# A two-layer audio trunk on one core: gates, norms and decays between the K, V and Q products, the output gate's products inside the chunk scan

## The reference

```
h = rms_norm(x, mix_norm_pre) @ mix_w_in          # Q,K,V,Z: 4 heads x 128 each; a,b: 4 each; conv part: 2 x 512
o_gdn = gated_deltanet_group(h, ...)
o_cm  = conformer_conv_group(h, ...)
x = x + rms_norm(concat([o_gdn, o_cm]) @ mix_w_out, mix_norm_post)

def gated_deltanet_group(h, conv_w, a_log, dt_bias, out_g):
    qkv = silu(causal_depthwise_conv(h[..., Q0:Z0], conv_w))       # 4 taps
    q = l2_normalize(qkv[:, :, 0]) * (128 ** -0.5)
    k = l2_normalize(qkv[:, :, 1]);  v = qkv[:, :, 2]
    g = -exp(a_log) * softplus(a + dt_bias);  beta = sigmoid(b)
    o = chunk_gated_delta_rule(q, k, v, g, beta)
    o = o * rsqrt(mean(o * o) + eps) * out_g
    return o * silu(z)

# chunk_gated_delta_rule: per chunk of tokens
#   decay = exp(gc_i - gc_j) on and below the diagonal (gc: cumulated g), a_mat = (beta k k^T * decay), strictly lower
#   (u, w) = (I + a_mat)^-1 (beta v, beta k exp(gc));  qk = q k^T * decay
#   scan: v_new = u - w S;  o = q exp(gc) S + qk v_new;  S = exp(g_last) S + (k exp(g_last - gc))^T v_new

def conformer_conv_group(h, dw_w, dw_b, ln_g, ln_b):
    glu = h[..., G0:G0+512] * sigmoid(h[..., G0+512:])
    u = causal_depthwise_conv(glu, dw_w) + dw_b                    # 31 taps, 512 channels
    return silu(layer_norm(u, ln_g, ln_b))
```

## Time and profile before

| | us |
|---|---|
| median of 3 runs | 2206.53 (2206.37 to 2212.68) |
| the profiled execution | 2205.52 |
| its span | 2203.8 |
| PE busy | 2099.9 (95%) |
| DVE busy | 1239.1 (56%) |
| ACT busy | 682.8 (31%) |
| POOL busy | 38.9 (2%) |

### The profile page before, as it was taken

The page is one execution under the profiler, slowest core; times in us unless marked ns, Lnnn a source line. Parts: engine busy times, 40 slices in busy tenths (PEclk is TensorE's granted clock), DMA queues, the critical chain, the costliest instruction groups (busy, mean ns, idle before and its releaser), DMA issues.

```text
span 2203.8 us, 26235 instructions
## 1 busy us (share of the span) xinstructions
PE 2099.9 (95%) x10044; PEld 1756.1 (80%) x10044; DVE 1239.1 (56%) x1707; ACT 682.8 (31%) x914; POOL 38.9 (2%) x51
## 2 busy tenths in 40 slices
PE   7999999997988999999999999999979799999997
PEld 6888887875887788888788888878758778888886
DVE  5555422899855755542375554258988656555323
ACT  5222222434225422222242222233341343222222
POOL 0000000000010000000000000000010000000000
PEclk9999999998999999999999999999979999999997
DMA  5333333223001233333233333323220023333320
GB/s 160 104 95 95 98 95 93 77 77 86 1 1 58 77 99 99 97 87 97 84 96 96 95 93 97 97 67 92 81 58 1 1 67 100 99 97 93 96 79 39
DMA packets 345792, 177.54 MB, mean 81 GB/s; under 512 B 8338, under 2 KB 344692, under 8 KB 345716
## 3 DMA queue, kind: packets, MB, share of 16 engines
q1 hardware_dynamic: 344058, 176.34, 28.0%
q10 hardware_dynamic: 1658, 0.16, 0.1%
HBM read 174.38 MB, written 2.10 MB: 80 GB/s over the span
## 4 chain that ended last, share of the span: by engine, by line
PE 77%; DVE 17%; ACT 3%; issue 2%; DMA 0%; DVEq 0%; SPq 0%; ACTq 0%
PE res L457 21%; PE res L459 21%; PE res L458 21%; DVE u L1301 7%; DVE cacc L1385 2%; PE res L521 1%; PE res L522 1%; PE pq L692 1%; PE stat L464 1%; PE res L525 1%; DVE wl L1137 1%; PE bc L485 1%; DVE pre L1371 1%; PE pq L457 1%; PE pq L459 1%
## 5 line engine op out<-in xcount | busy, mean ns | idle before, releaser
L818 ACT ACTIVATE wh<-raw 128x1024 fp32r<-128x1024 f32 (+1 forms) x336 | 347.8, 1037 | 1014.0 <-PE res L459 993.1
L1137 DVE TENSOR_TENSOR wl<-raw,wh 128x1024 fp32r<-128x1024 f32 (+1 forms) x336 | 401.8, 1197 | 392.6 <-ACT wh L818 392.2
L457 PE MATMUL res<-xh,wh 128*128 128x512 f32 x1576 | 614.2, 390 | 3.0 <-DVE xl L1151 3.0
L458 PE MATMUL res<-xl,wh 128*128 128x512 f32 x1576 | 613.2, 389 | 0.0
L459 PE MATMUL res<-xh,wl 128*128 128x512 f32 x1576 | 613.2, 389 | 0.0
L457 PEld LDWEIGHTS res<-xh,wh 128*128 128x128 f32 x1576 | 295.8, 188 | 65.0 <-DVE wl L1137 2.5
L459 PEld LDWEIGHTS res<-xh,wl 128*128 128x128 f32 x1576 | 295.8, 188 | 61.6
L458 PEld LDWEIGHTS res<-xl,wh 128*128 128x128 f32 x1576 | 295.8, 188 | 61.2
L457 PE MATMUL res<-hh,wh 128*128 128x512 f32 x704 | 273.9, 389 | 0.0
L458 PE MATMUL res<-hl,wh 128*128 128x512 f32 x704 | 273.9, 389 | 0.0
L459 PE MATMUL res<-hh,wl 128*128 128x512 f32 x704 | 273.9, 389 | 0.0
(11 more groups left out here) (268 smaller groups left out, 1936.1 us busy)
## 6 DMA issues: line engine op xcount, KB each, us to landing
raw<-in_ffn_w_in SPq DMA_DIRECT2D x176, 512.0 KB, 3.8
raw<-in_ffn_w_out SPq DMA_DIRECT2D x64, 448.0 KB, 3.7
raw<-in_mix_w_in SPq DMA_DIRECT2D x48, 512.0 KB, 4.0
raw<-in_ffn_w_out SPq DMA_DIRECT2D x32, 512.0 KB, 3.8
raw<-in_mix_w_out SPq DMA_DIRECT2D x16, 512.0 KB, 3.9
xin<-in_x SPq DMA_DIRECT2D x4, 512.0 KB, 5.0
out_dram<-xin SPq DMA_DIRECT2D x4, 512.0 KB, 4.0
crows<-in_cm_dw_w ACTq DMA_DIRECT2D x1, 62.0 KB
```

The source lines that it names most:

```text
L457: pe.matmul(bank, wh[:, slot, j, :], hi, start=first, stop=False)
L458: pe.matmul(bank, wh[:, slot, j, :], lo, start=False, stop=False)
L818: act.activation(wh[:, slot, 0:nk, :], raw[:, slot, 0:nk, :], ACT.Copy).then_inc(hi_full, 1)
L1137: dve.tensor_tensor(wl[:, slot, 0:nk, :], raw[:, slot, 0:nk, :], wh[:, slot, 0:nk, :].bitcast(F32), ALU.subtract).then_inc(lo_full, 1)
```

## The change

- The input phase computes K, V and Q only (r = 8 to 19). The 4 Z units are cut into 32 triples, and `z_tiles` places them in the scan: 2 before each product with `Xd`, 2 after it, 2 at a chunk's end, and twice 4 behind the last chunk. DVE's scaling of Z (`z_unit`) and the weights of the first output units (`refill`, `z_refill`) move with them.
- The product for a and b (`abT`) goes from after r = 15 to before r = 8; its copy goes to ACT. The softplus chain stands after the fourth K unit, K's norms after r = 13, the gates' sums after r = 15, the decays' products between r = 16 and r = 19, their Exp on ACT after the first Q unit.
- ACT applies the first of the 4 short taps. It also scales the decays by beta and the squared norm factor (`decay_scaled`), and turned V by the norm (`turned_tile`). K is no longer normalised by itself: the product for the system is K with K, and `kbT`, with its two turns and copies, is gone.
- The upper mask is a bf16 product of `identb` with `never` (-32768 below the diagonal) that opens the accumulation of the decays' exponents. POOL has nothing to do in the mixer.
- V and K are turned in the levels 1 to 4 of the inverse, one head after P(g=0) and one after Q(g=0) (4 PE turns and 4 ACT copies each).
- System, first level and scores are interleaved head by head.
- The taps of the long convolution: 22 in `glu`, 28 in K, V and Q, 2 before the inverse, 54 in the inverse (9 per level), and 18 in the scan's chunks 0 and 1. The channel sums for the layer norm are 16 PE matmuls over all four tiles (`token_sums`), where POOL had added the tiles and PE took 4.

The core of the diff:

```diff
...
-                    pool.tensor_tensor(Dm[:, h], Dm[:, h], upper[:].unsqueeze(1).broadcast_to([P, NC, P]),
...
+            pool.memset(never[:], 0.0).then_inc(s_seed, 1)
+            pool.memset(identb[:], 0.0).then_inc(s_seed, 1)
...
+            pool.affine_select(out=never[:], in_=never[:], compare_op=ALU.is_ge, fill=-32768.0, base=0,
+                               pattern=[[1, P]], channel_multiplier=-1).then_inc(s_mask, 1)
+            pool.affine_select(out=identb[:], in_=identb[:], compare_op=ALU.not_equal, fill=1.0, base=0,
+                               pattern=[[-1, P]], channel_multiplier=1).then_inc(s_mask, 1)
...
-                mixer_units(6, MIX_IN_U - 8)
+                mixer_units(6, 8)
                 pe.wait_ge(wab_ready, l * 2 + 2)
+                pe.wait_ge(rs_ready, l * 3 + 2)
...
-                mixer_units(MIX_IN_U - 8, MIX_IN_U - 4)
+                mixer_units(8, 10)
...
-                mixer_units(MIX_IN_U - 4, MIX_IN_U)
+                mixer_units(10, 14)
...
+                pe.wait_ge(na_ready, l + 1)
+                pe.wait_ge(l2_sq, l * 2 * H + H)
+                for h in range(H):
+                    mm = norms(128, ksqK, h)
+                mm.then_inc(l2_full, 1)
+                mixer_units(14, 16)
...
+                pe.matmul(stat[:, 160:176], lowst[:], gt["g"][:, 0:16], start=True, stop=True).then_inc(gc_full, 1)
...
+                def decays(h):
+                    bank = three[h % 3]
+                    if h == 0:
+                        pe.wait_ge(s_mask, 3 + 2 * 6 + 2)
+                    pe.wait_ge(w_ready, l * H + h + 1)
+                    pe.matmul(bank.rearrange("p (c t) -> p c t", c=NC), identb[:],
+                              never[:].unsqueeze(1).broadcast_to([P, NC, P]), start=True, stop=False)
+                    pe.matmul(bank, lowst[:], Wd[:, h].rearrange("p c t -> p (c t)"), start=False,
+                              stop=True).then_inc(e_full, 1)
+                mixer_units(16, 17)
+                decays(0)
+                decays(1)
+                mixer_units(17, 18)
+                decays(2)
+                mixer_units(18, 19)
+                pe.wait_ge(d_exp, l * H + 1)
+                decays(3)
+                mixer_units(19, 20)
+                    pe.wait_ge(mix_free, l * MIX_IN_U + Z_U - H + h + 1)
...
+                        mm = pe.matmul(in_bank(head_bank(h, l))[:, s], kT[:, h, s], kT[:, h, s], start=True, stop=True)
+                    mm.then_inc(kk_full, 1)
...
+                scores(0)
+                scores(1)
+                turn_u(0)
+                scores(2)
+                turn_u(1)
+                q_norms(0)
+                q_norms(1)
+                scores(3)
+                turn_u(2)
+                q_norms(2)
+                q_norms(3).then_inc(q2_full, 1)
+                turn_u(3)
...
+                        if g == 0 and 1 <= n < 5:
+                            turn_tile(2 * n - 2)
...
+                def z_tiles(n):
+                    for _ in range(n):
+                        r, k = Z_U + z_at[0] // KD, z_at[0] % KD
+                        z_at[0] += 1
+                        if k == 0:
+                            if r >= Z_U + 2:
+                                pe.wait_ge(mix_free, l * MIX_IN_U + r - 1)
+                            pe.wait_ge(lo_full, l * UNITS + MBASE + r + (1 + SLOTS))
+                        mm = tile(res[:, r % 2, :], r % SLOTS, k, xh[:, k, :], xl[:, k, :], k == 0, k == KD - 1)
+                        if k == KD - 1:
+                            mm.then_inc(unit_done, 1)
...
+                        pe.wait_ge(o_free, l * NC + c)
+                        for h in range(H):
+                            pe.matmul(res[:, 2, h * P:(h + 1) * P], qT[:, h, s], St[:, h, :], start=True, stop=True)
+                    z_tiles(2)
                     pe.wait_ge(xd_ready, l * NC + c + 1)
                     for h in range(H):
                         mm = pe.matmul(pq[:, 1, h * P:(h + 1) * P], Um[:, h, c, :], Xd[:, h, :], start=True,
                                        stop=True)
                     mm.then_inc(vn_full, 1)
+                    z_tiles(2)
...
+                    z_tiles(2)
                     if c == 1:
...
-                        token_sums(lacc[:]).then_inc(vsum_full, 1)
+                        pe.wait_ge(u_ready, l + 1)
+                        for t in range(CT):
+                            mm = token_sums(u[:, t, :], first=t == 0, last=t == CT - 1)
+                        mm.then_inc(usum_full, 1)
...
+                z_tiles(4)
+                for t in range(CT):
+                    pe.wait_ge(usq_ready, l * CT + t + 1)
+                    mm = token_sums(glu[:, t, PADC:], first=t == 0, last=t == CT - 1)
+                mm.then_inc(vsum_full, 1)
+                z_tiles(4)
+                pe.wait_ge(udiag, l + 1)
+                spread_column(rcol).then_inc(uvbc_full, 1)
...
+                def first_tap(n):
+                    w0 = C_QKV + (1, 2, 0)[n // H] * H + n % H
+                    act.wait_ge(mix_free, l * MIX_IN_U + 2 * CT + n + 1)
+                    act.activation(cacc[:, n % 2, :], pre[:, 0:T], ACT.Copy,
+                                   scale=call[:, l, w0:w0 + 1]).then_inc(tap0_ready, 1)
+                def activate(n):
...
+                def decay_scaled(h):
+                    act.wait_ge(br_ready, l + 1)
+                    act.wait_ge(d_exp, l * H + h + 1)
+                    for c in range(NC):
+                        n = h * NC + c
+                        ins = act.activation(Dm[:, h, c, :], Dm[:, h, c, :], ACT.Copy, scale=gt["br"][:, n:n + 1])
+                    ins.then_inc(d_ready, 1)
...
+                    first_tap(n)
+                    if n < H:
+                        act.activation(Um[:, n], ident[:].unsqueeze(1).broadcast_to([P, NC, P]),
+                                       ACT.Copy).then_inc(ui_ready, 1)
+                    high(MBASE + r + SLOTS, r % SLOTS, 8, l)
+                    if n == 0:
+                        act.wait_ge(abT_full, l + 1)
+                        act.activation(abT[:], bc[0:2 * H, :], ACT.Copy).then_inc(abT_ready, 1)
+                    activate(n)
+                    if n == 3:
+                        softplus()
...
+                    if n == 8:
+                        act.wait_ge(l2_full, l + 1)
+                        act.wait_ge(gc_full, l + 1)
+                        act.activation(gt["ss"][:, 0:16], stat[:, 128:144], ACT.Sqrt,
+                                       bias=eps[:, 0:1]).then_inc(l2_root, 1)
+                        act.activation(gt["egc"][:, 0:16], stat[:, 96:112], ACT.Exp)
+                        act.activation(gt["egl"][:, 0:16], stat[:, 112:128], ACT.Exp)
+                        act.activation(gt["ekd"][:, 0:16], stat[:, 160:176], ACT.Exp).then_inc(ekd_ready, 1)
+                        for h in range(H):
+                            decay(h)
+                    if n == 9:
+                        decay_scaled(0)
+                        decay_scaled(1)
+                    if n == 10:
+                        decay_scaled(2)
+                        decay_scaled(3)
...
+                    if c:
+                        z_refill(c - 1)
+                    if c < 3:
+                        o_square(c)
...
+                z_refill(3)
...
+                def qkv(n, first, second, third):
+                    r, which = 2 * CT + n, (1, 2, 0)[n // H]
+                    if n:
+                        dve.wait_ge(cv_ready, l * 3 * H + n)
+                    unit_out(r, pre[:, PADG:])
+                    conv_taps(first)
+                    dve.wait_ge(tap0_ready, l * 3 * H + n + 1)
+                    mark = 0
+                    for k in range(1, GTAPS):
+                        w = call[:, l, C_QKV + k * 3 * H + which * H + n % H:C_QKV + k * 3 * H + which * H + n % H + 1]
+                        if k > 1:
+                            st.need(mark)
+                        ins = dve.scalar_tensor_tensor(cacc[:, n % 2, :], pre[:, k:k + T], w, cacc[:, n % 2, :],
+                                                       ALU.mult, ALU.add)
+                        if k < GTAPS - 1:
+                            mark = st.done(ins)
+                            if k == 1:
+                                conv_taps(second)
+                            else:
+                                refill(r)
                         else:
...
-                                mark = st.done(dve.tensor_scalar(cacc[:, n % 2, :], src, w, None, ALU.mult))
...
-                                conv_taps(1)
...
-                        conv_taps((7, 6, 4, 2)[n])
...
-                conv_taps(9)
...
+                            ins.then_inc(cv_ready, 1)
+                    conv_taps(third)
+                taps = [(1, 1, 1), (1, 1, 1), (1, 1, 0), (1, 1, 1),
+                        (1, 1, 1), (1, 1, 0), (1, 0, 0), (1, 0, 0),
```

(37 more changed lines are left out.)

528 lines of the change are left out of this document (218 added, 310 removed).

## The result

The changed kernel takes 2225.0 us (median of 5 runs, 2221.4 to 2227.6); the kernel before 2206.5. The ratio is 1.0078, with a 95% interval of 1.006 to 1.0096: slower by 18.5 us. I had forecast 2194 with a range of 2179 to 2209. The result lies outside it and on the other side of zero.

A forecast was written before the change was run, and what follows sets the result against it. PE bounds the input phase, with DVE holding it up behind Z. Terms of -33.5, +0.5, +24.9, +1.5 and +0.3 give -6.3 us a layer, -12.6 for two: 2194 us, range 2179 to 2209.

The forecast's parts named there:

- VectorE's waits: Input phase: DVE stands from 503.1 before unit 9, some 7 us, waiting for ACT's decays and first tap.
- the fourth Exp: Input phase: ACT's last decay waits for PE behind input unit 18 and comes at about 510 us.
- first level: Start of the inverse: between 542.2 and 547.1 us, taken as 544.5, against 577.99 before.
- the sums of K: Input phase: K's norms add 4 x 0.82 = 3.3 us to PE's work.
- level 0: First level of the inverse: 9.5 us, within an inverse of 60.8 us against 60.3.
- The gain of 33.5 us: Stretch up to the inverse: its start moves from 577.99 to 544.5 us, -33.5 a layer.
- Levels 1 to 4: Inverse: added turns make the loop PE's, about 10.2 us a level instead of 9.4.
- The scan: Last inverse copy to turned heads: 64.4 us against 39.5, +24.9 a layer; Z's 21.7 us not hidden.
- 1.5 us for the clock: Scan: +1.5 us a layer for a lower clock behind the idle 3.2 us in chunk 1.
- Rival 3: Scan: clock stays low through half of the 32 triples, +10.9 us a layer, 2216 us; chance 0.15.
- Rival 1: Preparation, chunk 2 and tail: full clock holds, 6.0 us more gained a layer, 2182 us; chance 0.17.
- a drain behind each table load: ACT's three late table loads on the path: 3 us a layer more, 2200 us; chance 0.04.

The follow-up runs named there:

- e_ksplit: Changed kernel with the 16 one-column products that sum K's squares put in four places, half an input unit apart; 2217.3 us.
- e_fill_nq: e_fill with Q's 16 one-column norm products a layer replaced by 4 of four columns (values wrong); 2198.8 us.
- e_fill: Changed kernel with 26 and 22 spare products in TensorE's two gaps, ahead of K with K of the last head and ahead of the scores; 2214.3 us.
- e_notaps: Changed kernel without the 18 taps in chunks 0 and 1 of the scan; 2210.1 us.
- c2: c1 with Q's norms apart and Z's last three triples moved behind the spread of u's factors; 2180.6 us.
- e_usum: Changed kernel with the wait for u and its 16 sums put behind chunk 2's state products instead of in front; 2217.5 us.
- e_order: Changed kernel with ScalarE's fourth decay put behind the first tap of unit 9 instead of in front; 2224.4 us.
- c1: Changed kernel with Z triples in TensorE's gaps and singly in the scan's waits, K's and Q's norms spread, sums of u in two halves; 2185.3 us.
- b_fill: Kernel before the change with 46 spare 128x512 products in TensorE's gap ahead of the decays; 2214.0 us.

## Why the prediction was wrong

**The input phase, as forecast, bar its clock.** VectorE's waits came where I put them: 7.49 us at unit 9 (ahead of 513.85; I had 503.1 to 511), the fourth Exp at 512.61 (510), first level at 547.59 (542.2 to 547.1, taken 544.5). It stands half a microsecond above my upper bound. My lower bound was added up wrong: 539.6 and the four steps behind it, 3.17 us, make 542.8, not 542.2. I priced the sums of K by their work, 3.3 us, and not by the 6.7 us of half clock around and behind them. From 473.26 to 490.96 these sums and two units took 17.7 us where 3.3 and 10.9 would do: 3.5 us, as much as this term missed, and in e_ksplit the clock holds there.

**The inverse: the step that failed.** I wrote 9.5 us for level 0, which presumes the full clock; it took 17.0. The gain of 33.5 us had been made by thinning TensorE's work ahead of the first level: V's and K's turns gone, gaps of 6.59 and 5.45 us, then scores and one-column sums. The kernel before has K with K and Q with K one behind the other from 567.06 and enters level 0 at full clock. I considered the clock for the preparation itself and for the scan, and not for the stage after. That the time went by what stood ahead of level 0, and not by level 0 itself, e_fill_nq shows: 9.6 us in both layers. Levels 1 to 4 took 10.13 us each, forecast 10.2.

**The scan: mechanism right, size short.** Chunks 0 and 1 ran as counted, TensorE idled before the sums of u (2.94; I had 3.2 with the wait counted from idle), and Z was not hidden. I had 1.5 us for the clock; the sums alone took 6.26 instead of 3.3 us, and the first half of output unit 0 stood at the half clock that I had allowed for. Together 4.3 short. My price of a gap was also read from one row where there are two: the kernel before has a second gap of 1.77 us, and behind it the same product took 1.16 us, not 1.84:

```profile
662.64 1.16 PE L730 MATMUL pq<-Xd,Um 128*128 128x128 f32 x8 [1.77 <-DVE Xd L1500]
```

**The rivals.** Rival 3, the slower one, named the right resource in the wrong place: triples at 1.2 GHz in the scan. The level before it fell instead. Rival 1, a clock that holds everywhere, is what e_fill_nq comes nearest to, but only after changes, and its clock still falls in the scan. I gave a drain behind each table load (the Trainium skill, ScalarE: Activation LUTs, What ACT_TABLE_LOAD costs) 4 in 100, and the trace after disagrees with it as well: the load at 504.39 took 1.28, and the next operation started at 505.69. Three drains of 1.38 us are 4.1 us a layer, an estimate from that page, and not the 3 that I wrote.

**What the rule would have said.** I had quoted the Trainium skill (TensorE: Matmul & The Clock Gate, Part 1), "the default state is throttled, and activity releases the throttle", and used it only for a rival in which Z's triples hold the clock up. The trace agrees with that use: without most of them the scan's granted clock is 0.72 and 0.74 instead of 0.88 and 0.84. Read in the other direction it speaks against the change: what thins TensorE's work ahead of a stage that TensorE bounds can be paid for in that stage. The sentence alone doesn't give the size: level 0 kept TensorE busy throughout and stayed at 0.50 for 14 us.

**Open.** That the clock took the time of level 0 is shown, and that the two gaps are enough for it. What lowers it where the gaps are filled is not. One-column sums in a row were followed by a fall at 473.26 and in layer 0 of e_fill, and by none in layer 1 of e_fill, in e_notaps, and in the kernel before, where 16 of them stand between turns from 562.40 on. Whether their columns, the weight loads beside them or the small products around them matter wasn't separated, and c2's level 0 fell without such a row. The same instructions also run differently from one execution to the next: from the start of layer 0's mixer to K with K the kernel after took 136.1 us and e_fill and e_usum 133.5, with nothing edited there, and the kernels after and e_order range over 6 and 15 us from run to run. What decides that is not shown, so a few microseconds between two single traces carry no cause.

## What to carry to other kernels

Price a stage of small products on TensorE twice, by its work and by the clock that it leaves to the next stage; a busy share of 100% at a granted clock of 0.50 is the sign. Spend movable wide work (here a projection) in the gaps ahead of the stage that TensorE bounds, not beside a chain that has little room; here that and the spreading of the one-column sums gave 39.7 us in one step (c1), though not a full clock everywhere. Before you call a pattern the cause of a low clock, look whether it does the same in every layer of the same trace. When VectorE comes off the path, ask at what clock TensorE will take over.

## What the runs showed of the hardware

- 16 float32 sums of one column (32 records) in a row, in the kernel after at 473.26: 4.22 us of busy TensorE, and from about 476 to 482.6 us 1.2 GHz without any idle time. In groups of four, half a unit apart (e_ksplit): 0.95 us a group, clock 1.00. In a row, in e_notaps at 631.84: 3.63 us, clock 1.00 behind them.
- 46 fp32r products of 128x512 behind a gap of 3.03 us (b_fill): 13.3 us in layer 0 and 11.8 in layer 1, where 46 x 0.226 would be 10.4.
- The clock can stay down without any idle time: in the kernel after, level 0 is at 0.50 from 548 to 562 us with TensorE busy throughout.
- The same instructions can meet either clock: level 0 of e_fill took 15.5 us in layer 0 and 9.6 us in layer 1.
